# A block of 18 stages on one core: residual by token, weights moving in 512 columns

## The reference

```python
def rms_norm(x, g):                      # x: 256 tokens x 1024
    y = x * rsqrt(mean(x * x, -1) + 1e-6)
    return y * g
def adaln(x, g, shift, scale):
    return rms_norm_2(x, g) * (1 + scale[:, None, :]) + shift[:, None, :]
def swiglu(h, w_in, w_out):              # 1024 -> 2 x 2816 -> 1024
    a, b = jnp.split(h @ w_in, 2, axis=-1)
    return (jax.nn.silu(a) * b) @ w_out
...
mod = (c_act @ ada_w[i] + ada_b[i])      # shift, scale and gate of each sublayer
x = x + MACARON_W * gate[:, 0, None] * swiglu(h, ffn_w_in[i, 0], ffn_w_out[i, 0])
...
# experts: 32 of 128 hidden units, two of them chosen per token, weights cw (computed densely)
hid = silu(einsum('td,edf->tef', xt, w_gate)) * einsum('td,edf->tef', xt, w_up)
y = einsum('tef,efd->td', hid * cw[:, :, None], w_down)
```

## Time and profile before

| | |
|---|---|
| three timed executions | 3965.15, 3969.73, 3976.12 us |
| profiled execution, its own time | 3968.26 us |
| its span | 3966.3 us |
| mean granted clock of TensorE | 0.972 |
| PE busy | 3727.6 us (94%), 28914 matmuls |
| DVE busy | 2674.1 us (67%) |
| ACT busy | 1738.8 us (44%) |
| POOL busy | 743.7 us (19%) |
| read from HBM | 659.38 MB, 167 GB/s over the span |

### The profile page before, as it was taken

One profiled execution on the slowest core, in us unless ns is written; L12 is line 12 of the kernel. 1 busy time (PEld: TensorE's weight loads), 2 busy tenths in 40 slices (PEclk: granted clock), 3 DMA queues, 4 the chain that ended last, 5 costly groups with the idle time before them and its releaser, 6 DMA issues.

```text
span 3966.3 us, 68495 instructions
## 1 busy us (share of the span) xinstructions
PE 3727.6 (94%) x28914; PEld 3462.0 (87%) x28914; DVE 2674.1 (67%) x4778; ACT 1738.8 (44%) x2951; POOL 743.7 (19%) x555
## 2 busy tenths in 40 slices
PE   7999999999999889989999989999999998889899
PEld 7779998799989767789998969999979998777799
DVE  4567876688677665567777776777667765665554
ACT  3353344533454443344545644444454544433343
POOL 2024442244300421110002420000100002322100
PEclk9899999999999899999999999999999999999999
DMA  5126753277567310057674416767437663300142
GB/s 208 70 80 242 270 197 123 92 275 266 195 246 267 104 70 1 1 192 273 237 273 162 146 54 236 271 232 276 154 128 273 236 258 132 101 17 1 63 177 107
DMA packets 64113, 664.83 MB, mean 168 GB/s; under 512 B 7104, under 2 KB 7616, under 8 KB 8512
## 3 DMA queue, kind: packets, MB, share of 16 engines
q1 hardware_dynamic: 63808, 660.46, 44.6%
HBM read 659.38 MB, written 1.05 MB: 167 GB/s over the span
## 4 chain that ended last, share of the span: by engine, by line
PE 68%; DVE 21%; ACT 7%; issue 2%; POOL 1%; DMA 0%; SPq 0%; DVEq 0%; ACTq 0%; POOLq 0%
PE pb L273 66%; DVE wp L226 6%; DVE ring L243 4%; ACT wp L264 3%; DVE sq L226 2%; PE pb L280 2%; DVE wk L238 2%; DVE wk L226 2%; DVE sq L238 1%; ACT sq L264 1%; DVE hT L238 1%; ACT wk L264 1%; DVE rsb L226 1%; ACT ex L264 1%; POOL sq L226 0%
## 5 line engine op out<-in xcount | busy, mean ns | idle before, releaser
L273 PE MATMUL pb<-hx,wp 128*128 128x256 f32 x15360 | 1935.0, 286 | 77.7 <-DVE hx L238 37.6
L273 PEld LDWEIGHTS pb<-hx,wp 128*128 128x128 f32 x15360 | 1892.9, 194 | 99.4 <-issue 78.2
L226 DVE TENSOR_TENSOR wp<-ring,wp 128x1024 fp32r<-128x1024 f32 (+1 forms) x847 | 1021.3, 1240 | 351.7 <-ACT wp L264 350.9
L264 ACT ACTIVATE wp<-ring 128x1024 fp32r<-128x1024 f32 x936 | 937.8, 1046 | 212.0 <-PE pb L273 207.8
L226 POOL TENSOR_TENSOR wp<-ring,wp 128x512 fp32r<-128x512 f32 (+1 forms) x243 | 484.2, 2006 | 1610.4 <-ACT wp L264 1568.8
L273 PE MATMUL pb<-ex,wp 128*128 128x256 f32 x5856 | 748.0, 285 | 20.0 <-DVE ex L226 17.5
L273 PEld LDWEIGHTS pb<-ex,wp 128*128 128x128 f32 x5856 | 723.7, 193 | 25.5 <-DVE ex L226 17.9
L243 DVE CUSTOM_DVE_ANT_0 ring<-ring,cact,prm 128x1024 f32<-128x1024 f32 x288 | 418.6, 1501 | 0.0
L273 PE MATMUL pb<-wk 128*128 128x128 f32 (+8 forms) x3008 | 388.3, 293 | 22.0 <-ACT wk L264 6.9
L273 PEld LDWEIGHTS pb<-wk 128*128 128x128 f32 (+4 forms) x3008 | 286.3, 172 | 115.8 <-issue 45.4
L264 ACT ACTIVATE sq<-pb 128x256 f32<-128x256 f32 (+1 forms) x216 | 88.4, 409 | 669.6 <-PE pb L273 600.0
(11 more groups left out here) (186 smaller groups left out, 2709.3 us busy)
## 6 DMA issues: line engine op xcount, KB each, us to landing
ring<-weights SPq DMA_DIRECT2D x385, 1536.0 KB, 6.7
ring<-weights SPq DMA_DIRECT2D x41, 1024.0 KB, 4.9
ring<-weights SPq DMA_DIRECT2D x4, 512.0 KB, 9.6
cst<-consts SPq DMA_DIRECT2D x1, 2032.0 KB, 10.6
ring<-weights SPq DMA_DIRECT2D x1, 1280.0 KB, 5.5
ring<-weights SPq DMA_DIRECT2D x1, 1152.0 KB, 5.0
xT<-xT_in SPq DMA_DIRECT2D x1, 1024.0 KB, 4.8
xT_out<-xT SPq DMA_DIRECT2D x1, 1024.0 KB, 3.9
```

Source lines behind the costliest of these rows:

```text
L226: return self.real.tensor_tensor(out, a, b, op) if self.real else Uncounted()
L264: return self.real.activation(out, a, func, bias=bias, scale=scale, accum_out=accum)
L273: return self.real.matmul(out, l, r, start=start, stop=stop, skip_group_check=skip)
```

## The change

**Operands change places.** In the output projections of all mixers, in the gated stages and in ple the activations become the stationary operand (128 features x 128 tokens) and the weights move, 512 columns at a time (`mm3_tokens`). The outputs, and with them the residual (`xt`, 2 tiles of 128 tokens x 1024), lie by token. The input projections of the mixers stay as they were (weights stationary, 256 tokens moving).

**Gated stages in steps.** The unit is now a pair p of the former units (256 hidden values), and a step s is a pair and one of the two token tiles t. A step has 24 matmuls for gate and up (`gate_up`), after the second of the eight k-tiles of which the gated product of the step before is turned (`turn`: two transposes of 128x128, because the down product needs it by feature), and the 12 matmuls of the down product of the step two before (`whole_down`). A pair's weights are two chunks: A with three pieces of its gate and up weights, B with the fourth and the two down pieces of the pair before. A modulation chunk comes in every odd step of pairs 0 to 9 (feed-forward stages 6 to 15) or 2 to 14 (experts).

**Norms by tile.** The new class `Head` takes the norm of one token tile after the other: ACT sums squares along a row, DVE and ACT take the root of a 128x1 column, DVE scales the first 512 features and ACT the rest, PE transposes eight 128x128 tiles into PSUM, and ACT and DVE apply gain and shift there and make the halves. `boundary_act`, `boundary_dve` and `boundary_pe` put the end of a stage and the head of the next into one order. Early weight pieces of the next stage are split in between.

**Other parts.** The residual update of a modulated stage takes two DVE operations on 512 columns (times the gate row, then added); the gate row is brought to all partitions by two DMAs on SP's queue (`load_gate`). The logits of the experts are taken from the finished norm, and the experts' weights are scalars per token, so the spreads go. Low halves of weights in gated stages are DVE's, except in the first pairs of an expert stage.

Counts of the two programs: PE instructions 26093 before and 17129 after; of these 12672 + 5856 + 576 matmuls of 256 columns go and 9552 of 512 columns come; transposes of 128x128 go from 640 to 1408; low halves of 128x1024 on DVE from 693 to 813, on POOL from 89 (and 154 of 128x512) to 33 (and 90); DMAs on SP from 446 to 483.

```diff
+    def mm3_tokens(e, out, x, w, start, stop):
+        e.mm(out, x[0], w[1], start, False, skip=True)
+        e.mm(out, x[0], w[0], False, False, skip=True)
+        return e.mm(out, x[1], w[0], False, stop, skip=True)
...
+        def turn(*steps):
+            bk.hold(e, 7, (st, "hid", steps[-1]), (x_lo, (st, "hid", steps[-1])))
+            for s in steps:
...
+                    e.wait_ge(*v_out[st, "glu", s])
+                for j in range(2):
+                    ins = e.tp(turned_at(g, s)[:, j * 128:(j + 1) * 128], sg[s % 4][:, j * 128:(j + 1) * 128])
...
+        def gate_up(s, between={}):
+            p, t = divmod(s, 2)
...
+            for k in range(KD):
+                w = g.gu[p][k // 2]
+                split_ready(e, w)
+                e.wait_ge(*x_lo[st, "h", t, k])
+                ins = mm3_tokens(e, ps[:, :], tok_hx(k, t), [a[:, (k % 2) * 512:(k % 2 + 1) * 512] for a in (w.hi, w.lo)],
+                                 k == 0, k == KD - 1)
...
+        second_tokens = {4: lambda: head.pe(e, 1)}
...
+        else:
+            gate_up(0, second_tokens)
+            gate_up(1, {1: lambda: turn(0)})
+        for s in range(6 if g.routed else 2, last):
+            gate_up(s, {1: lambda: turn(s - 1)})
+            whole_down(s - 2)
+        gate_up(last, {1: lambda: turn(last - 1)})
+        down(last - 1, 0)
+        turn(last)
+        down(last - 1, 1)
+        for hf in range(2):
+            down(last - 2, hf)
+            down(last, hf)
+        boundary_pe(e, st)
...
+        for s in range(6 if g.routed else 0, last + 1):
+            modulations(s)
+            here = 1 if s % 2 == 0 and s else 0
+            split_lo_v(e, g.split[s][:here])
+            if s:
+                low(s - 1)
+            split_lo_v(e, g.split[s][here:])
+            if s == last - 1:
+                split_lo_v(e, early(st + 1)[:2])
+            up(s)
+        boundary_dve(e, st, update, IN_TURN, (), [lambda: low(last)])
...
+    def boundary_act(e, st, pieces=None, middle=()):
+        h, now = head_of(st + 1), early(st + 1)
+        split_hi(e, now[:2] if pieces is None else pieces)
+        for step in middle:
+            step()
+        if h is None:
+            return
+        e.tables("natural_log_exp_and_others")
+        split_hi(e, now[2:3])
+        h.square_act(e, 0, 0)
+        split_hi(e, now[3:])
+        h.square_act(e, 0, 1)
+        h.root_act(e, 0)
+        h.unit_act(e, 0)
+        h.square_act(e, 1, 0)
+        h.halves_act(e, 0)
+        h.square_act(e, 1, 1)
+        h.root_act(e, 1)
+        h.unit_act(e, 1)
+        h.halves_act(e, 1)
...
+        def update(t, hf):
+            e.wait_ge(*product[st, "out", t, hf])
+            e.wait_ge(s_gate, 32 * (n + 1))
+            x, ps = X2[:, t, hf * 512:(hf + 1) * 512], pb[2 * t + hf][:, :]
+            p3 = ps.rearrange("p (k n) -> p k n", k=4)
+            e.stt(p3, p3, scale, gate_rows[:, hf * 4:(hf + 1) * 4, :], ALU.mult, ALU.mult).then_inc(
+                *v_step.up((st, "gated", t, hf)))
+            e.wait_ge(*v_step[st, "gated", t, hf])
+            e.tt(x, x, ps, ALU.add).then_inc(*x_new.up((st, t, hf)))
```

More of the change, by code:

```diff
@@ L1839, in dve @@
[L1839 to L1851 removed]
+        l_gate, l_proj = [None, None], [None, None]
```

1192 lines of the change are left out of this document (639 added, 553 removed).

## The result

The changed kernel takes 4073.18 us (median of 4 runs, 4060.54 to 4086.71), the one before beside it 3969.5 us (median of 4). The ratio is 1.026, with a 95% interval of 1.0224 to 1.0296: slower by 104 us, where 3851 us and a gain were forecast. The profiled execution has a span of 4071.8 us.

The account below looks back on a forecast made before the run. The prediction took PE as the bound, mostly the pair of a load and a short matmul; its terms summed as 3968.3 - 218 + 56 - 40 + 47 + 33 + 5 = 3851 us, range 3775 to 3945 for eight in ten.

Parts of the forecast that it names:

- Term 1: Matmuls with 512 moving columns: 19104 at 120 ns become 9552 at 216 ns, taken as -218 us.
- the nearest row is the 512-cycle pass, which I take: Wide matmul's price, 216 ns, taken from a single-precision pass of 256 columns, measured at 215 ns.
- No change: Rival: wide matmuls start near 228 ns apart, so the kernel's time stays the same; chance 0.04.
- The rate of the moving operand: Rival: reading the moving operand holds wide matmuls at 240 ns, giving 4069 us; chance 0.11.
- Term 2: Gated stages: two transposes of the gated product in each of 240 steps, 0.235 us a pair, +56 us.
- Term 3: Two expert stages: spreads of expert weights go and most waits at start and end vanish, -40 us.
- Term 4: Loop between DVE and the weight ring: PE waits 0.45 us per pair, 0.6 in expert stages, +47 us.
- the chunk lands 6.7 us after its issue: Modulation chunk's landing time in the weight ring, used to work out when DVE gets it.
- the loop is loose: Rival: modulation chunks land later, 96 x 1.0 us more, giving 3947 us; chance 0.16.
- Term 5: Stage boundaries with norms taken tile by tile: longer chains and more products at the lower clock, +33 us.
- +2 each, +9 for four: Boundaries before mixers that need both token tiles before they start: 2 us more at each.
- a stage over 199 us: Sign: feed-forward stages were forecast at 195 us; one over 199 would make the whole forecast wrong.

Follow-up runs that it names:

- e3: e1 with every 512-column matmul of the gated stages issued as two of 256 columns; 4068.55 us, ratio 1.0248.
- e4: The changed kernel with eleven rows of 48 matmuls of several widths and precisions added behind its last product; one execution, read in its trace.
- e1: The changed kernel with each modulation chunk put between weight chunks A and B of the next pair in the ring's order; 3974.34 us, ratio 1.0021.
- e2: The changed kernel with the weight chunk behind each modulation chunk issued only when that modulation chunk has landed; 4100.54 us, ratio 1.033.
- e6: e1 with three changes of ACT's and DVE's order at stage boundaries, among them tile 1's last update earlier before mixers; 3952.49 us, ratio 0.996.
- e8: e6 with the first unit's silu and product earlier in feed-forward stages, and the gate row written in feature order; 3930.93 us, ratio 0.9907.
- e9: e8 with filler matmuls on constants put into PE's waits at stage boundaries; 3922.52 us, ratio 0.9886.

## Why the prediction was wrong

The forecast was -117 us, the result +104: 221 us apart. In the order of its terms:

**Term 1, the width, mis-sized.** It was to give 218 us and gives 104 (e3 scaled to all). The step that failed is "the nearest row is the 512-cycle pass, which I take": that pass is single precision and pays 3 ns beside its cycles, while each reduced-precision matmul pays 13 at any width from 256 columns on (e4). The 120 ns of the earlier trace rows were read as the loading of the stationary operand, with the earlier trace rows as the proof. But the load takes 111 ns, less than 120, and so was hidden at 256 columns too. Columns plus 13 ns would have given 120 and 227, and that reading was open. The prediction had it only as the rival "*No change*, a spacing near 228" with a chance of 0.04; it came true as to the spacing, with the other losses on top. The rate of the moving operand (240 ns, the rival on the other side) fell too. The rule of the Trainium skill that was weighed there, 2.5 ns beside the columns, holds for the single-precision rows of e4 and not for the reduced-precision ones. About 114 us of the gap. With the 60 us of the turns against it, the change of operands is worth 44 us and not 162, so there was little to lose before the whole became slower.

**Term 2, the turns, right.** 0.24 to 0.26 us a pair against 0.235: about 60 us against 56.

**Term 3, the experts, about right.** With the loop gone (e1) the two expert stages take 35 us less than before. The width gives 2 x 32 x 36 x 12 ns = 28 of that and the turns take 16, so 23 are left for the waits, with the boundary at the stages' heads in it; forecast were 40 - 7 = 33. About 10 us of the gap.

**Term 4, the loop, right in mechanism and half its size.** +47 were forecast, e1 gives back 99. The step that failed is "the chunk lands 6.7 us after its issue": it takes 7.6 us in the median and up to 9.9. The rest of the way round, from the landing to the next issue, follows from the prediction's times as 12.2 + 0.45 - 2.9 = 9.75 us, and 9.97 were measured. With PE's pair at 16.83 us instead of 16.0 the loop takes 17.81: 1.0 us lost per pair, not 0.45. A later landing was seen (the bound of 1.5 us per pair, and the rival "the loop is loose", 0.16), so the size came about, but not by the reason that was given for the rival, that another chunk follows at once: with one behind and none ahead a chunk lands in 6.4 us (e1), with none behind and one ahead in 8.3 (e2). The lateness goes with a chunk ahead that is still in flight; its exact cause stays open. About 52 us of the gap.

**Term 5, the boundaries, too small.** What remains of the gap, some 40 us, is here and in the clock. PE's waits for norms went from 100 to 173 us, +73, where the term had +33 and the start +5. A feed-forward boundary with its head behaves as worked out: in e1 stage 14 takes 198.4 us, 185.0 of it 22 steps of 8.41, so 13.4 are lost against 14.0 forecast. The mixers and gate stages are where the term failed: they take 58 us more, though wide output products save them some 10 by estimate (912 matmuls x 12 ns). The step was "+2 each, +9 for four" before the mixers (four times 2 is 8, a slip without weight), taking two tiles one after the other for the same chain as one tile of both. Ahead of stage 13 on PE, before and in e1, the first product of the mixer comes at these times (the start of the norm's sums was 2810.87, the start of tile 0's transposes is the first line of the second group):

```profile
2818.02 1.32 PE L273 MATMUL pb<-hx,wp 128*128 128x256 f32 x6 [0.33 <-DVE hx L238]
```

```profile
2805.27 1.03 PE L279 MATMUL pb<-cst,sq 128*128 128x128 f32 x8
...
2821.74 18.48 PE L272 MATMUL pb<-hx,wp 128*128 128x256 f32 x152
```

From the start of the last product ahead of the norm to this first product it was 7.6 us and is 16.7. For the five mixers with both tiles needed (stages 3, 7, 10, 13, 16) the traces give 12.6, 13.5, 13.4, 7.6 and 13.5 us before, 60.5 together, and 26.9, 18.6, 19.8, 16.7 and 13.4 in e1, 95.5 together: +35 where +9 stood. Before these mixers tile 1's last update stood behind tile 0's work on DVE, which gave a wait of 9 us at stage 13. e6 moves it and e8 makes the update shorter; e8 has 85.0 us in these five places. Orders and stride give 43 us back in all (e1 to e8), 39 of them in the feed-forward stages by the division used above (1544.0 us in e8) and 10 in the mixers and gate stages (1799.1), so most of what these lost is still there in e8. How it divides between chains and clock was not taken apart.

**The clock.** Mean 0.958 instead of 0.972, 120 us more at the lower level. By the clock's records 69 us of them lie where PE is busy and 50 where it stands still, so they cost at most some 35 us and not 60, and e9 got back 8.

The forecast that a stage over 199 us would make the whole wrong has come true (211.9). Rightly named were the place of the waits (turned units, only with modulation chunks, ended by DVE) and that POOL bounded nothing.

## What to carry to other kernels

Take the price of a matmul as columns plus a fixed part and get the fixed part from two widths of the same precision; a row of another precision does not prove which of two reasons an excess has. Where a ring of buffers feeds an engine that also frees them, follow the time round the ring, and put a chunk that is needed on a tight schedule right behind the slot that comes free first: here one place in the order was worth 99 us of 4073. Take the time of a landing from rows in which as many chunks are in flight as will be. When a norm is split by tiles, look at what the next stage needs first: where it needs both tiles, work on the first that stands before the last update of the second on the same engine is on the way (moving it, with two other changes of order, gave 22 us in e6).

## What the runs showed of the hardware

- A reduced-precision matmul with a full stationary operand starts every 227 to 229 ns at 512 columns, 175 at 384, 120 to 122 at 256 and 112 at 128 (e4). A single-precision pass of 256 columns starts every 216.
- Of two transfers of 1.5 MB issued 0.4 us apart the first landed in 6.4 us (e1, median of 66 with nothing in flight ahead), as if alone. Issued 4.65 us after another that was still in flight, a transfer took 8.8 us (3052.77, changed kernel) and 9.1 (3078.93, e2, with nothing behind it); not every one in that position was late (6.4 us for 51 weight chunks of e1), and the cause is not shown. Waiting for one before issuing the other gained nothing (e2).
- A DVE operation on 512 numbers per partition whose second operand has a stride of 32 bytes took 1.12 us, with a stride of 4 bytes 0.69 (e8). The Trainium skill ("SBUF — State Buffer", section "Door 1: The DMA port swizzle (why `[64,N]` ≈ `[32,N]`)") says that SBUF has lines of 16 bytes and that each step to another line pays; the two rows agree with that, which I had not looked up when I priced the update at 0.69.
- Time at the lower clock is a poor measure of loss: 87 us less of it brought 8 us (e9), and 52 of them had been time in which TensorE stood still.
